# Layer 2's second modulation part: its eight pieces taken out of layer 1's merges and run between the two layers

## The chip, the cores and the metric

One Trainium2 chip, one core. The kernel is one program; the metric is its time on the device in microseconds, the median of several executions.

## What is computed

A diffusion backbone of two layers over 256 latent tokens and 256 context tokens, D = 1024. Each layer computes six modulation vectors, runs three token mixers behind one input projection, merges them by gates, and then a grouped mixture of 16 experts. Cut to what bears on this case:

```python
for l in range(DEPTH):
    ml = (silu(c) @ w_mod[l] + b_mod[l]).reshape(b, 1, N_MOD, d)          # w_mod[l]: 1024 x 6144
    mc = (silu(c_ctx) @ w_mod[l] + b_mod[l]).reshape(1, 1, N_MOD, d)
    hl = modulate(rms_norm(xl, norm1_g[l]), ml[:, :, 0], ml[:, :, 1])
    hc = modulate(rms_norm(xc, norm1_g[l]), mc[:, :, 0], mc[:, :, 1])
    out_l, out_c = token_mixers(hl, hc, w_in[l], ...)
    xl = xl + ml[:, :, 2] * out_l
    hl2 = modulate(rms_norm(xl, norm2_g[l]), ml[:, :, 3], ml[:, :, 4])
    ...
    f = grouped_moe(tokens, w_router, router_bias, w_gate_e[l], w_up_e[l], w_down_e[l])
    xl = xl + ml[:, :, 5] * f[:b * s].reshape(b, s, d)
    ...
```

The modulation depends on `c`, `c_ctx` and the weights alone, so layer 2's may be computed at any time before it is used.

## The kernel before

The layers are counted from 0 in the code: layer 1 of this text is `l == 0`, layer 2 is `l == 1`. Every engine has a program written out by hand (`block.sync` for SP, which issues the weight loads; `block.gpsimd`, `block.tensor`, `block.scalar`, `block.vector`), and they meet only in semaphores. Each engine does its list in order; a wait holds up all that stands behind it on that engine. SP loads weights chunk by chunk, 1 MB each, into a ring of three slots; the order of the chunks is a list (`order`), and `mod_behind` says behind which chunk a modulation piece is loaded.

**Modulation.** `w_mod` of a layer is 24 pieces of 128 x 2048 (1 MB), three parts (i = 0, 1, 2) of eight pieces (k = 0 to 7). Part 0 is shift and scale of the first norm, part 1 the gate of the mixers' output and the shift of the second norm, part 2 the scale of the second norm and the gate of the experts. A piece is `mod(l, i, k)` (L1032 to L1049): TensorE multiplies `csil` (silu of c and of c_ctx, 32 columns wide) with four blocks of 512 columns, into four row groups of one bank, and sums over k. Then ScalarE copies the bank (`mod_rows`), TensorE turns it by four transposes (`mod_columns`), VectorE adds the bias (`mod_take`). For layer 2 the pieces are loaded by `mod_piece` into places of their own (`mod_places`), mostly one buffer, `mod_next`, so that SP waits for `m_us` (pieces used) before it loads the next.

**Where layer 2's pieces run before.** In layer 1's merges. These are 3 branches (n) of 8 tiles (m). A tile is `gate` (8 steps over k, `mm3` = three products each, lines L1020 to L1022) and `branch` (4 steps), 36 products of 128x128 by 512 columns. `next_mod(1)` stands behind tiles 0, 3 and 7 of n = 0, behind all of n = 1 and behind the first five of n = 2: 16 pieces, part 0 and part 1. Part 2 follows behind the output projection and in the second norm.

**Experts and combine of layer 1.** After the last expert product, TensorE has work for layer 2's long filters: `filters`, `spectra_a`, `spectra_b` (products with `dft_f`, L1079 and L1097), and between them `keep_busy`, products of constants (`ones` by a constant table, L1011) whose results nobody reads. Meanwhile GpSimd gathers each token's first-choice rows (L908), stores the last expert's rows (L904), waits for all stores, signals `z_r`, and gathers the second-choice rows (L940): four gathers of 512 KB each, one for each 128 tokens. ScalarE scales the first choices, VectorE adds the second choices (L2909, `z_f`). TensorE then transposes the rows, column k into bank k (L1727); VectorE adds them to the stream `xT` (L2917, `z_x`), ScalarE squares, and TensorE sums the squares (L1004) for layer 2's first norm. Behind that stand `filters(l, 1)`, five more products of constants, and the first three tiles of layer 2's projection, run side by side (`in_bank`).

```python
                    spectra_b(l + 1, 0)
                    keep_busy(1, 5)
                    pe.wait_ge(f_a[l + 1], 6 * l + 10)
                pe.wait_ge(z_f[l], 4 * l + nt)
                pe.wait_ge(x_ya[l], 16 * l + NS)
                pe.wait_ge(x_yd[l], 16 * l + NS)
                for k in range(DK):
```

## Time and profile before

| | |
|---|---|
| median of 3 runs | 1567.48 us (1567.27 to 1571.9) |
| the profiled execution | 1569.26 us, its span 1567.6 us |
| TensorE busy | 1471.8 us, 94% of the span |
| VectorE, ScalarE, GpSimd | 877.5, 632.7, 406.1 us |
| DMA | 362.78 MB, mean 231 GB/s over the span |
| merges of layer 1 | about 362 to 510 us; out projection to 592 |
| last expert product of layer 1 | about 937 us |
| first projection product of layer 2 | 978.66 us |

How to read it: times are microseconds from the span's start. TensorE's products are pipelined, so their durations overlap and the distance from one start to the next is what a product costs. A row that starts with an engine's name and a line says what the engine did there, and behind it, in brackets, how long it had idled and whose work ended that. "PEclk" is the TensorE clock that was granted, as a share of 2.4 GHz. The DMA rows tell two queues apart: SP's (hardware) and GpSimd's (software); both use the same 16 DMA engines.

### The profile page before, as it was taken

The page shows a single profiled execution, that of the slowest core. Times are in us where ns is not written, and L with a number is a line of the kernel's source. Part 1 is how long each engine was busy: PE and PEld are TensorE (multiplying, and loading weights), DVE is VectorE, ACT ScalarE, POOL GpSimd, SP SyncE. Part 2 cuts the span into 40 slices and gives each one's busy share as a digit, 9 for nine tenths or more (in the row PEclk, how much of TensorE's full clock was granted, in tenths as well). Part 3 has the DMA queues.
Part 4 walks back from the last instruction along what each step waited for, and adds up shares of the span by engine and source line. Part 5 has one row for each costly group of instructions (what it writes and reads, how often), then busy time and mean ns, then how long its engine had stood idle before and what let it go on. Part 6 is the DMA issues. An engine that isn't in the chain of part 4 may idle for free.

```text
span 1567.6 us, 20695 instructions
## 1 busy us (share of the span) xinstructions
PE 1471.8 (94%) x8212; PEld 1086.9 (69%) x8212; DVE 877.5 (56%) x1266; ACT 632.7 (40%) x853; POOL 406.1 (26%) x367
## 2 busy tenths in 40 slices
PE   6999999899999997899999999999988997999997
PEld 2588788657777784678888874697868995445444
DVE  4725556774222347799999967664783566111112
ACT  2532222264222335477787755442264443010102
POOL 0446334201333440111101013473414661000000
PEclk9999999999999998899999999998999999999997
DMA  8423211376456573799999983252304766899993
GB/s 330 147 81 107 81 55 59 133 279 223 160 191 205 190 277 126 267 370 403 406 409 405 397 314 122 65 185 81 102 22 152 259 233 276 329 420 420 422 421 133
DMA packets 116898, 362.78 MB, mean 231 GB/s; under 512 B 7774, under 2 KB 73632, under 8 KB 85952
## 3 DMA queue, kind: packets, MB, share of 16 engines
q1 hardware_dynamic: 109296, 334.62, 56.5%
q0 software_dynamic: 7504, 26.81, 4.6%
q8 instruction: 67, 1.10, 0.3%
q14 instruction: 31, 0.25, 0.0%
HBM read 349.86 MB, written 11.53 MB: 231 GB/s over the span
## 4 chain that ended last, share of the span: by engine, by line
PE 49%; DVE 10%; issue 2%; ACT 1%; DMA 0%; POOL 0%; DVEq 0%; PEldq 0%; ACTq 0%
PE bank L1020 9%; PE bank L1021 9%; PE bank L1022 9%; PE bank L1540 7%; PE bank L1579 4%; PE bank L1493 2%; PE bank L1479 1%; PE bank L1549 1%; PE bank L1504 1%; PE bank L1097 1%; PE bank L1231 1%; PE bank L1606 1%; PE bank L1011 1%; PE bank L1607 1%; DVE mix L2403 0%
## 5 line engine op out<-in xcount | busy, mean ns | idle before, releaser
L833 POOL TENSOR_TENSOR w_lo<-ring,w_hi 128x256 fp32r<-128x256 f32 (+1 forms) x300 | 347.8, 1188 | 515.0 <-ACT w_hi L1864 515.0
L1020 PE MATMUL bank<-h_hi,w_hi 128*128 128x512 f32 (+1 forms) x768 | 272.1, 354 | 8.8 <-POOL w_lo L833 3.4
L1021 PE MATMUL bank<-h_hi,w_lo 128*128 128x512 f32 (+1 forms) x768 | 263.1, 343 | 0.0
L1022 PE MATMUL bank<-h_lo,w_hi 128*128 128x512 f32 (+1 forms) x768 | 263.0, 342 | 0.0
L1020 PEld LDWEIGHTS bank<-h_hi,w_hi 128*128 128x128 f32 x768 | 146.5, 191 | 41.1 <-issue 16.5
L1021 PEld LDWEIGHTS bank<-h_hi,w_lo 128*128 128x128 f32 x768 | 146.6, 191 | 16.8 <-issue 1.4
L1022 PEld LDWEIGHTS bank<-h_lo,w_hi 128*128 128x128 f32 x768 | 146.5, 191 | 16.8
L1020 PE MATMUL bank<-w_hi,h_hi 128*128 128x512 f32 (+1 forms) x384 | 141.8, 369 | 6.7 <-DVE h_lo L2785 3.1
L1864 ACT ACTIVATE w_hi<-ring 128x1024 fp32r<-128x1024 f32 x120 | 125.4, 1052 | 40.5 <-PE bank L1020 31.4
L1021 PE MATMUL bank<-w_hi,h_lo 128*128 128x512 f32 (+1 forms) x384 | 138.1, 360 | 0.0
L1022 PE MATMUL bank<-w_lo,h_hi 128*128 128x512 f32 (+1 forms) x384 | 137.7, 359 | 0.0
L2561 DVE SCALAR_TENSOR_TENSOR mix<-mix,bank 128x512 f32<-128x512 f32 (+1 forms) x48 | 26.5, 553 | 168.5 <-PE bank L1022 116.7
L1020 PEld LDWEIGHTS bank<-w_hi,h_hi 128*128 128x128 f32 x384 | 74.1, 193 | 17.7 <-issue 3.7
L2043 ACT ACTIVATE mix<-bank 128x256 f32<-128x256 f32 (+1 forms) x39 | 18.8, 481 | 165.9 <-PE bank L1022 164.2
L2617 DVE TENSOR_TENSOR w_lo<-ring,w_hi 128x2048 fp32r<-128x2048 f32 x32 | 73.3, 2292 | 17.4 <-ACT w_hi L2073 17.4
L1022 PEld LDWEIGHTS bank<-w_lo,h_hi 128*128 128x128 f32 x384 | 74.0, 193 | 10.8
L1021 PEld LDWEIGHTS bank<-w_hi,h_lo 128*128 128x128 f32 x384 | 74.1, 193 | 10.4 <-issue 0.5
L2617 DVE TENSOR_TENSOR w_lo<-mix,w_hi 128x2048 fp32r<-128x2048 f32 x32 | 73.1, 2284 | 2.3 <-ACT w_hi L2073 2.3
L2073 ACT ACTIVATE w_hi<-mix 128x2048 fp32r<-128x2048 f32 x32 | 61.4, 1918 | 22.1 <-PE bank L1022 22.1
L994 POOL TENSOR_SCALAR mix<-xT,fin_g 128x256 f32<-128x256 f32 x4 | 3.6, 919 | 253.8 <-DVE xT L2917 253.8
L2073 ACT ACTIVATE w_hi<-ring 128x2048 fp32r<-128x2048 f32 x32 | 61.2, 1915 | 19.3 <-PE bank L1022 19.3
L1540 PE MATMUL bank<-operands_plain,mix 128*64 128x512 f32 x248 | 63.9, 594 | 0.0
(367 smaller groups left out, 2865.6 us busy)
## 6 DMA issues: line engine op xcount, KB each, us to landing
ring<-in_w_in SPq DMA_DIRECT2D x52, 1024.0 KB, 5.0
mix<-in_w_gate_e SPq DMA_DIRECT2D x40, 1024.0 KB, 7.8
ring<-in_w_up_e SPq DMA_DIRECT2D x38, 1024.0 KB, 8.1
mix<-in_w_down_e SPq DMA_DIRECT2D x25, 1024.0 KB, 8.3
ring<-in_w_mod SPq DMA_DIRECT2D x24, 1024.0 KB, 6.0
ring<-in_w_down_e SPq DMA_DIRECT2D x23, 1024.0 KB, 7.5
mix<-in_w_mod SPq DMA_DIRECT2D x19, 1024.0 KB, 4.9
operands_plain<-in_w_up_e SPq DMA_DIRECT2D x16, 1024.0 KB, 12.3
```

The source lines that it names most:

```text
L833: last = pool.tensor_tensor(w_lo[:, slot, k:k + n], rview(raw, 8)[:, k:k + n, x * P:(x + 1) * P], w_hi[:, slot, k:k + n].bitcast(F32), ALU ...
L1020: first = mm(dst, stat[0], mov[0], start=start, stop=False)
L1021: mm(dst, stat[1], mov[0], start=False, stop=False)
L1022: return first, mm(dst, stat[0], mov[1], start=False, stop=stop)
L1493: last = mm(bank[i][:, k * P:(k + 1) * P], htok[:, j, (4 * i + k) * P:(4 * i + k + 1) * P], hot_rows[l][e % 2][:, j, :], start=j == 0, sto ...
L1540: last = mm(dst[x * M:(x + 1) * M, :], heT[:, 0, 4 * h + k, x * M:(x + 1) * M], raw(l, c)[:, k * FF:(k + 1) * FF], start=h + k == 0, stop= ...
L1579: last = mm(y_bank[o][x * M:(x + 1) * M, :], hidT[:, 0, 2 * h + k, x * M:(x + 1) * M], raw(l, c)[:, k * D + o * 512:k * D + (o + 1) * 512] ...
L1864: A(w_hi[:, slot], rview(raw, 8)[:, :, x * P:(x + 1) * P], ACT.Copy).then_inc(w_h, 1)
L2043: A(gate_t[:, m % 2, 0:T], gate_v, ACT.Tanh, scale=0.5).then_inc(g_t[l], 1)
L2073: A(xhi[c % XH], raw(0, c), ACT.Copy).then_inc(x_wh, 1)
L2561: last = V.scalar_tensor_tensor(gated, gate_t[:, m % 2, 0:T], 1.0, bank[2 + m % 2][:, 0:T], ALU.add, ALU.mult)
L2617: V.tensor_tensor(xlo[c % XH], raw(0, c), xhi[c % XH].bitcast(F32), ALU.subtract).then_inc(x_wd, 1)
```

## The change

Part 1 of layer 2 no longer runs in layer 1's merges. The order of the parts becomes 0, 2, 1 (`nth`). In the merges, n = 1 keeps pieces behind its first five tiles, n = 2 has none. Six pieces of part 1 take the place of the five products of constants before the row transposes; two more stand behind `filters(l, 1)`, where five products of constants become three. The part's eight loads (`late_piece`, nine DMAs) stand in SP's list behind layer 2's first three ring chunks: the first four wait for the last expert product of layer 1 (`x_u`), the fifth for `z_r`, the seventh for the sixth to be used. They land in `plain` (the area of the operands), `mix` and `mod_next`. Since the part now holds bank 6 until layer 2's first tiles are done, the third tile goes to bank 7, the sizes of the second filter to bank 5, and row column 6 to bank 1, behind a wait for VectorE. ScalarE's copy stands behind layer 2's first norm, the four transposes behind the third tile, VectorE's add behind the taps.

```diff
@@ -302,7 +302,9 @@
         ropes = [v.rearrange("p (i t) -> p i t", i=2) for v in rope_at]
         tidx = sb("tidx", [P, 64], U32)
 
-        mod_places = ([mod_next] * (2 * DK) + [ahead[:, 0:2048], mod_next] + [plain[:, 2048 * i:2048 * (i + 1)] for i in range(4)]
+        late_places = [[plain[:, 2048 * i:2048 * (i + 1)]] for i in (1, 3, 0, 2)]
+        late_places += [[area(0, 2048)], [mod_next], [mod_next], [plain[:, o + 3072:o + 4096] for o in (8192, 12288)]]
+        mod_places = ([mod_next] * DK + late_places + [ahead[:, 0:2048], mod_next] + [plain[:, 2048 * i:2048 * (i + 1)] for i in range(4)]
                       + [area(o, 2048) for o in (4096, 8192)])
         didx = sb("didx", [P, 2, 4], U32)
         counts = sb("counts", [P, 8], U32)
@@ -487,12 +489,23 @@
             return mods[:, i:i + n, s] if l == 0 else mods_next[:, MOD_T * s + i:MOD_T * s + i + n]
 
         def transforms_to(l):
-            return 16 * (4 + l * (2 + MOD_C))
+            return 16 * (4 + l * (2 + 2 * DK))
 
         def acc(k):
 
             return bank[4 + k // 2][:, k % 2 * SEQ:(k % 2 + 1) * SEQ]
 
+        def nth(l, i):
+
+            return 3 * l + (0, 2, 1)[i] if l else i
+
+        def late_sem(j):
+
+            return j % len(x_full)
+
+        def late_to(j):
+            return 16 * (EXP_C // len(x_full) + j // len(x_full) + 1)
+
         def mbank(l, i):
 
             return bank[7 if l == 0 and i else 5 + i % 2]
@@ -505,9 +518,17 @@
 
             return 6 + v % 2 * l
 
-        def in_bank(g):
-
-            return bank[6 if g == 2 else g % 2]
+        def in_bank(l, g):
+
+            return bank[6 + l if g == 2 else g % 2]
+
+        def size_bank(l, o):
+
+            return bank[5 if l and o else 7]
+
+        def row_bank(k):
+
+            return bank[1 if k == 6 else k]
 
         fbank = [[bank[i] for i in (2, 3, 4, x)] for x in (0, 5)]
 
...
@@ -730,7 +752,7 @@
             def mod_piece(p):
 
                 if p:
-                    sp.wait_ge(m_us, min(p, 2 * DK))
+                    sp.wait_ge(m_us, min(p, DK))
                 else:
                     sp.wait_ge(a_o[0], len(units_of[0]))
                 if p == 3 * DK - 1:
@@ -739,10 +761,22 @@
                 sp.dma_start(mod_places[p], a["w_mod"][1, k * P:(k + 1) * P, i * RW:(i + 1) * RW]).then_inc(s_lds, 16)
 
 
+            def late_piece(j):
+
+                if j == 0:
+                    sp.wait_ge(x_u, EXP_C)
+                elif j == 4:
+                    sp.wait_ge(z_r, 1)
+                elif j == 6:
+                    sp.wait_ge(m_us, 2 * DK + j)
+                n = RW // len(late_places[j])
+                for i, place in enumerate(late_places[j]):
+                    sp.dma_start(place, a["w_mod"][1, j * P:(j + 1) * P, RW + i * n:RW + (i + 1) * n]
+                                 ).then_inc(x_full[late_sem(j + i)], 16)
+
             base = at_of[("out", 0, 0)] - MERGE_C
             mod_behind = {base + 4: [0, 1], base + 6: [2], base + 8: [3], base + 9: [4, 5, 6],
-                          base + 11: [7], base + 12: [8, 9, 10], base + 14: [11], base + 15: [12, 13, 14],
-                          base + 17: [15], base + 18: [16, 17], base + 21: [18, 19, 20, 21, 22, 23]}
+                          base + 11: [7], base + 18: [16, 17], base + 21: [18, 19, 20, 21, 22, 23]}
 
 
             once_behind = (6, 9, 12)
@@ -783,6 +817,9 @@
                         filter_tables(l + 1)
                     for p in mod_behind.get(at, []):
                         mod_piece(p)
+                    if l and at == lo + RS - 1:
+                        for j in range(DK):
+                            late_piece(j)
                     if l and kind == "merge" and i in once_behind:
                         expert_load(l, once_behind.index(i))
                 for c in range(len(once) if l else 0, EXP_C):
...
@@ -1037,14 +1074,20 @@
 
                     pe.wait_ge(j_a[l], TAKEN)
                 if l:
-                    pe.wait_ge(s_lds, transforms_to(0) + 16 * (DK * i + (DK if i == 2 else k + 1)))
+                    if i == 1:
+                        for j in range(k, k + len(late_places[k])):
+                            pe.wait_ge(x_full[late_sem(j)], late_to(j))
+                    else:
+                        pe.wait_ge(s_lds, transforms_to(0) + 16 * (2 * DK if i else k + 1))
                     w = mod_places[DK * i + k]
+                    w = w if isinstance(w, list) else [w]
                 else:
                     at = at_of[("mod", l, DK * i + k)]
                     pe.wait_ge(ring_full[at % RS], full_at(at))
-                    w = ring[:, at % RS]
+                    w = [ring[:, at % RS]]
+                n = 4 // len(w)
                 for c in range(4):
-                    last = mm(mbank(l, i)[32 * c:32 * c + 32, :], csil[:, k, :], w[:, c * 512:(c + 1) * 512],
+                    last = mm(mbank(l, i)[32 * c:32 * c + 32, :], csil[:, k, :], w[c // n][:, c % n * 512:(c % n + 1) * 512],
                               start=k == 0, stop=k == DK - 1)
                 last.then_inc(m_us if l else ring_used, 1)
 
...
@@ -1137,13 +1180,15 @@
                         norm_sum(2 * l, NT, k)
                     pe.wait_ge(z_x[l - 1], 16 * l)
                     filters(l, 1)
-                    keep_busy(6, 5)
+                    keep_busy(1, 3)
+                    for k in range(DK - 2, DK):
+                        mod(l, 1, k)
 
                 def proj_steps(g):
 
                     cols = NT if 20 <= g < 24 else T
                     q = g if g < 24 else g - 4
-                    b = in_bank(g) if g < 12 else bank[g % 4 if g < 16 else 6 + g % 2]
+                    b = in_bank(l, g) if g < 12 else bank[g % 4 if g < 16 else 6 + g % 2]
                     abreast = g < ABREAST[l]
 
                     pe.wait_ge(w_l, q0 + q + 1)
@@ -1202,6 +1247,8 @@
                     if g >= ABREAST[l]:
                         proj_tile(g)
                     if g == 2:
+                        if l:
+                            mod_columns(l, 1)
                         spectra_a(l, 1)
                     if g == 3 - l:
                         spectra_b(l, 1)
@@ -1353,12 +1400,11 @@
                             first.then_inc(carry, 1)
                     last.then_inc(g_pe[l], done)
 
-                pieces = [0]
+                pieces = iter([(i, k) for i in (0, 2, 1) for k in range(DK)])
 
                 def next_mod(n):
-                    for p in range(pieces[0], pieces[0] + n):
-                        mod(1, p // DK, p % DK)
-                    pieces[0] += n
+                    for _ in range(n):
+                        mod(1, *next(pieces))
 
                 pe.wait_ge(a_o[l], U)
                 for n in range(3):
@@ -1382,10 +1428,10 @@
                         else:
                             branch(n, m, 1)
                             gate(n, m, g_pe[l], ring_used)
-                        if l == 0 and (n == 1 or m % 4 == 3 and n == 0 or n == 2 and m < 5):
+                        if l == 0 and (n == 1 and m < 5 or n == 0 and m % 4 == 3):
                             next_mod(1)
-                        if l == 0 and n and m == 6:
-                            mod_columns(1, n - 1)
+                        if l == 0 and n == 1 and m == 6:
+                            mod_columns(1, 0)
                     if n == 0 and l == 0:
                         pe.wait_ge(j_pe[l], 32 + DK)
                     else:
@@ -1712,7 +1758,8 @@
                     keep_busy(1, 4)
                     spectra_a(l + 1, 0)
                     spectra_b(l + 1, 0)
-                    keep_busy(1, 5)
+                    for k in range(DK - 2):
+                        mod(l + 1, 1, k)
                     pe.wait_ge(f_a[l + 1], 6 * l + 10)
 
                 if l:
@@ -1721,10 +1768,12 @@
                 pe.wait_ge(x_ya[l], 16 * l + NS)
                 pe.wait_ge(x_yd[l], 16 * l + NS)
                 for k in range(DK):
+                    if k == 6:
+                        pe.wait_ge(z_x[l], 16 * l + 4)
                     if k == DK - 1 and l + 1 < DEPTH:
                         pe.wait_ge(f_d[l + 1], 10 * l + 16)
                     for j in range(nt):
-                        last = tp(bank[k][:, j * P:(j + 1) * P], fa[j][:, k * P:(k + 1) * P], ident)
+                        last = tp(row_bank(k)[:, j * P:(j + 1) * P], fa[j][:, k * P:(k + 1) * P], ident)
                     last.then_inc(z_t[l], 1)
 
             rows_bank = [bank[2:4], bank[4:6]]
...
@@ -1877,6 +1926,8 @@
                     spectrum_b(l, 0)
                 act.wait_ge(m_d[l], 2 * l + 1)
                 norm_act_scale(2 * l, NT, 2)
+                if l:
+                    mod_rows(1, 1)
 
                 for g in range(12):
                     if g + AHEAD >= ABREAST[l]:
...
@@ -2357,12 +2408,14 @@
                 if l == 0:
                     gate_scales(0, 0)
                 taps(l, 1)
+                if l:
+                    mod_take(1, 1)
 
                 for g in range(12):
                     dve.wait_ge(j_c[l], 12 * l + g + 1)
                     dst = hv[:, g, 0:T] if g < 4 else hx[:, (g - 4) // 4, g % 4, 0:T]
                     dst = dst.rearrange("p (s t) -> p s t", t=SEQ)
-                    src = in_bank(g)[:, 0:T].rearrange("p (s t) -> p s t", t=SEQ)
+                    src = in_bank(l, g)[:, 0:T].rearrange("p (s t) -> p s t", t=SEQ)
                     link(V.scalar_tensor_tensor(dst[:, :, 1:SEQ], src[:, :, 0:SEQ - 1], pc[:, C_TAP + g:C_TAP + g + 1],
                                                 dst[:, :, 1:SEQ], ALU.mult, ALU.add))
                     V.scalar_tensor_tensor(dst[:, :, 0:SEQ - 1], src[:, :, 1:SEQ],
...
```

TensorE, from layer 2's first spectra to the first row transpose, before (L1011 are the products of constants, L1727 the transposes):

```order
L1092 MATMUL bank<-square,mix 128x1 x7
L1097 MATMUL bank<-mix,dft_f 128x512 [waits filter_act]
L1097 MATMUL bank<-mix,dft_f 128x512 x3
L1011 MATMUL bank<-square 128x512 x5
L1727 MATMUL bank<-square,gates_ahead 128x128 [waits expert_out_first,expert_out_second,combined,filter_act]
```

and with the change (L1090 is a piece, L1776 the transposes; `mix` and `operands_plain` are places of pieces):

```order
L1135 MATMUL bank<-square,mix 128x1 x7
L1140 MATMUL bank<-mix,dft_f 128x512 [waits filter_act]
L1140 MATMUL bank<-mix,dft_f 128x512 x3
L1090 MATMUL bank<-operands_plain,csil 32x512 [waits expert_weights_loaded0]
L1090 MATMUL bank<-operands_plain,csil 32x512 x3
...
L1090 MATMUL bank<-mix,csil 32x512 [waits expert_weights_loaded4]
L1090 MATMUL bank<-mix,csil 32x512 x3
L1090 MATMUL bank<-mix,csil 32x512 [waits expert_weights_loaded5]
L1090 MATMUL bank<-mix,csil 32x512 x3
L1776 MATMUL bank<-square,gates_ahead 128x128 [waits expert_out_first,expert_out_second,combined,filter_act]
```

Five products that wait for nothing have become six pieces, each of which waits for its load.

SP, at the start of its part for layer 2, before:

```order
L715 DMA mix<-in_hy_w 128x1024
L716 DMA mix<-in_decay 128x1024
L779 DMA ring<-in_w_in 128x8x256 [waits expert_weights_split]
L728 DMA poolw<-in_pool_w 128x4x128
L779 DMA ring<-in_w_in 128x8x256 [waits expert_weights_split] x2
L779 DMA ring<-in_w_in 128x8x256 [waits weight_half_split] x13
```

and with the change:

```order
L813 DMA ring<-in_w_in 128x8x256 [waits expert_weights_split] x2
L774 DMA operands_plain<-in_w_mod 128x2048 [waits expert_weights_used]
L774 DMA operands_plain<-in_w_mod 128x2048 x3
L774 DMA mix<-in_w_mod 128x2048 [waits expert_rows_all_stored]
L774 DMA mix<-in_w_mod 128x2048
L774 DMA mix<-in_w_mod 128x2048 [waits mod_piece_used]
L774 DMA operands_plain<-in_w_mod 128x1024 x2
L813 DMA ring<-in_w_in 128x8x256 [waits weight_half_split] x13
```

The nine loads stand between the third ring chunk and the fourth.

## Rows read from the trace of the kernel before

**Rows 1.** The page: TensorE's busy time, share of the span, instructions.

```profile
PE 1471.8 (94%) x8212; PEld 1086.9 (69%) x8212; DVE 877.5 (56%) x1266; ACT 632.7 (40%) x853; POOL 406.1 (26%) x367
```

**Rows 2.** Windows, merges of layer 1: length; PE, PEld, DVE, ACT, POOL; clock, DMA.

```profile
430.00:512.00 82.00, 82.00 (x389) 59.61 (x388) 19.97 (x25) 19.01 (x26) 26.62 (x32) 1.00 0.61 206
```

**Rows 3.** Timeline of PE, merges: start, duration, engine, line; L1047 pieces, L1029 transposes.

```profile
425.91 1.07 PE L1047 MATMUL bank<-mix,csil 128*32 128x512 f32 x8
...
435.30 1.07 PE L1047 MATMUL bank<-mix,csil 128*32 128x512 f32 x8
...
463.46 1.07 PE L1047 MATMUL bank<-mix,csil 128*32 128x512 f32 x8
464.45 0.66 PE L1029 MATMUL bank<-square,mix 128*128 128x128 f32 x4
...
473.24 1.07 PE L1047 MATMUL bank<-mix,csil 128*32 128x512 f32 x8
```

**Rows 4.** Timeline of PE, last expert product to layer 2's projection.

```profile
938.01 1.99 PE L1070 MATMUL bank<-mix 64*128 64x512 f32 x8 [0.75 <-PE bank L1022]
...
955.24 4.46 PE L1011 MATMUL bank<-square 128*128 128x512 f32 x10
959.53 0.49 PE L1727 MATMUL bank<-square,gates_ahead 128*128 128x128 f32 x3
...
963.06 7.70 PE L1004 MATMUL bank<-mix,square 128*128 128x512 f32 x16
...
972.61 4.56 PE L1011 MATMUL bank<-square 128*128 128x512 f32 x10
978.66 0.36 PE L1020 MATMUL bank<-h_hi,w_hi 128*128 128x256 f32 x1 [1.49 <-DVE h_lo L2254]
```

**Rows 5.** Timeline of POOL and DVE in the combine.

```profile
939.88 0.59 POOL L904 DMA_DIRECT2D y_rows<-mix  x1
947.32 1.60 POOL L940 DMA_INDIRECT mix<-y_rows,didx  x1 [6.84 <-DMA y_rows<-mix]
...
957.81 1.28 DVE L2909 SCALAR_TENSOR_TENSOR mix<-mix,wsel 128x1024 f32<-128x1024 f32 x1
...
961.46 6.36 DVE L2917 SCALAR_TENSOR_TENSOR xT<-bank,mods,xT 128x256 f32<-128x256 f32 x16
```

**Rows 6.** DMA queues (records, MB, engine share): 937-939.4, 939.4-957.5, 949.5-957.5, 874-876 us.

```profile
q0 software_dynamic: 180, 0.67, 94.4%
q0 software_dynamic: 1110, 4.02, 66.1%
q0 software_dynamic: 576, 2.10, 80.2%
q0 software_dynamic: 110, 0.42, 58.1%
q1 hardware_dynamic: 59, 0.37, 45.7%
```

**Rows 7.** Windows, SP's queue alone (last: GB/s); DMA issues, median us to landing.

```profile
554.00:558.00 4.00, 4.00 (x19) 3.06 (x18) 0.05 (x1) 1.66 (x2) 4.00 (x7) 1.00 1.03 427
...
mix<-in_w_mod SPq DMA_DIRECT2D x19, 1024.0 KB, 4.9
...
operands_plain<-in_w_mod SPq DMA_DIRECT2D x4, 1024.0 KB, 12.2
...
mix<-y_rows,didx POOLq DMA_INDIRECT x4, 5.8
```

**Rows 8.** Windows at the low clock (third number from the end), and spectra at either.

```profile
930.00:933.50 3.50, 3.50 (x9) 2.78 (x10) 0.00 (x0) 0.00 (x0) 0.00 (x0) 0.53 0.65 242
...
991.00:995.00 4.00, 3.90 (x5) 1.65 (x6) 3.97 (x3) 0.93 (x2) 4.00 (x2) 0.57 0.14 29
...
944.48 3.70 PE L1079 MATMUL bank<-mix,dft_f 128*128 128x512 f32 x8 [0.85 <-DVE mix L2316]
...
991.10 5.40 PE L1079 MATMUL bank<-mix,dft_f 128*128 128x512 f32 x8 [1.85 <-DVE mix L2316]
```

29 lines of the change are left out of this document (15 added, 14 removed).

## Prediction

> **What bounds the kernel now.** I read the page first, then the merges of layer 1 engine by engine, then the stretch between layer 1's last expert and layer 2's first projection, and last the DMA queues there, since the change takes work out of the first place and puts it into the second.
>
> TensorE is busy 94% of the span [rows 1]. In the merges, where the eight pieces of the second part run today, it is busy 82.00 of 82.00 us, while VectorE, ScalarE and GpSimd have 20, 19 and 27 us [rows 2]. So what is taken out there is gained in full. The reader should see in the timeline that one merge tile with a piece behind it takes 9.39 us (425.91 to 435.30), and that the tile which also has the four transposes behind it takes 9.78 (463.46 to 473.24) [rows 3].
>
> In the combine there are two chains. TensorE's own: last expert product before 938.0, the spectra, five products of constants (955.24, 4.46 us), then the row transposes at 959.53 and the sums of squares at 963.06 [rows 4]. Beside it the rows' chain: GpSimd stores the last expert rows (939.88), may gather the second choices only when all is stored (947.32), VectorE adds the last of them from 957.81 to 959.09, and the transposes wait for that [rows 5]. So TensorE's filling and the gathered rows end within half a microsecond of each other: either is the bound as soon as it grows. The DMA engines carry 0.67 MB of GpSimd's queue from 937 to 939.4 and 4.02 MB from 939.4 to 957.5, and nothing of note from SP's queue [rows 6]. That is the empty place that the change wants to fill.
>
> **Taken out of layer 1's merges.** A merge tile is 36 products, at the spacing of 0.227 us that the tile of 9.39 us leaves when a piece is set at 1.22: 36 x 0.227 = 8.17, and 9.39 - 8.17 = 1.22 us [rows 3]. Eight pieces are 9.76 us, and the four transposes 9.78 - 9.39 = 0.39 more: **-10.15 us**. I count it whole, since no other engine has even a third of the time there [rows 2]. ScalarE's copy, VectorE's add, and eight loads of 1 MB leave the stage too; nothing waited for them, so they give nothing. SP's ring loads are no longer queued behind the waits for these pieces, which gives nothing either where TensorE never idles.
>
> **Put into the combine: TensorE.** Six pieces in place of five products of constants. A piece is four narrow products side by side, 1.07 us from first to last [rows 3], 0.9 when they follow each other; a product of constants is 4.46 / 5 = 0.89 [rows 4]. That is 0.9 to 2 us more. It costs nothing of its own if the rows' chain has grown by more than that, which the next paragraph says. The last two pieces stand where two of the five products before the first projection stood (972.61, 4.56 us), and TensorE is 1.49 us early there [rows 4], so they are free as long as they have landed. They are issued once the sixth is used, and the sums of squares (7.7 us) and more lie in between, against 4.9 us to land [rows 4, 7].
>
> **Put into the combine: DMA.** This is the term that decides. SP may start the first four pieces when the last expert product is done, 937.3; with 4.9 us to land, of which 1.05 / 0.427 = 2.5 are transfer, their bytes begin at 939.7 [rows 4, 7]; the rows are split at 939.4, and I count from there. The fifth and the sixth go out with the signal that all rows are stored, which is also the gathers' start. All six, 6 x 1.05 = 6.29 MB, must have landed before the row transposes, because TensorE takes its work in order; the gathers must too. The order in which the two queues are served hardly matters, then: the later of them ends when 4.02 + 6.29 = 10.31 MB are through the same sixteen engines. What rate? GpSimd's queue alone keeps the engines over 90% busy at 0.28 MB/us (0.67 MB in 2.4 us) [rows 6]; SP's queue alone reaches 0.427 [rows 7]; where both run, as from 874 to 876, 0.42 and 0.37 MB pass in 2 us, 0.395 MB/us, with each queue holding about half of the time [rows 6]. This last row is the nearest, and I take it: 10.31 / 0.395 = 26.1 us, to 965.5. The bounds are 10.31 / 0.427 = 24.1 us (963.5) and 4.02 / 0.28 + 6.29 / 0.427 = 29.1 us (968.5). The last rows landed, 0.3 us for the signal, 1.28 for VectorE's add and 0.44 to the first transpose, as today [rows 4, 5], put the transposes at 967.5 instead of 959.53: **+8.0 us**, bounds 6.0 and 11.0.
>
> **The bank moved.** Row column 6 now goes into bank 1, which VectorE must have emptied. It starts its sixteen adds 1.93 us after the first transpose and takes 0.4 us for each [rows 4, 5], so four are done at +3.5; the two last columns (3.53 / 8 = 0.44 us each) follow, and the sums of squares start at +4.5 instead of +3.53: **+1.0 us**. Were the pieces last to land, not the rows, VectorE would be ahead and this would be 0.
>
> **The clock.** TensorE will wait for rows and for the sixth piece. Rows of both levels exist here: from 930 to 933.5 and from 991 to 995, the latter after TensorE had idled 1.85 us, the granted clock was 0.53 and 0.57, that is 1.2 GHz nearly all the time; the same eight products took 5.40 us at 991 in place of 3.70 at 944 [rows 8]. A second cause of idling: ScalarE scales the first-choice rows before it copies the spectra out, and TensorE's second spectra wait for that copy; first choices that land late will hold them up. At the transposes part of such a loss falls on time in which they wait for VectorE anyway. I take **+1.0 us**, between 0 and 4 (the sums of squares, 7.7 us at full clock, half of them at the low one).
>
> **Edits priced at nothing.** ScalarE's copy of the part stands after the norm, where it has nothing to do until the first tiles are done; the four transposes after the third tile stand in the 1.85 us in which TensorE waits for VectorE at 991.10 [rows 8]; VectorE's add of 16 numbers a partition stands before its first convolution, while TensorE runs the second spectra. SP's next ring chunk goes out behind the pieces, and its slot comes free only when GpSimd has split two halves, about when the sixth piece is used. Were these covers gone, the transposes would cost 0.39 us as in the merges, the copy and the add less than 1 us together.
>
> **Sum.** -10.15 + 8.0 + 1.0 + 1.0 = -0.15 us. The profiled execution took 1569.26 us, 1.8 more than the median of 1567.48; the difference is applied to the median: 1567.3, which I give as 1567.4. A measurement of this kernel can tell 0.3%, 4.7 us, from no change; so the forecast is **no change**.
>
> **The rule on the queues.** The rows show each queue with about half of the engines' time: 58% and 46% from 874 to 876, and GpSimd's 110 records of 3.8 KB against SP's 59 of 6.3 [rows 6]. The Trainium skill, DMA: Bandwidth & Descriptors, section "Queues, rings and completion order", says that an engine goes round the queues packet by packet, a packet being a group of descriptors. By that rule the share would go by the packets' sizes and not be a half; the row bears it out only in so far as neither queue is starved. It is rival B below.
>
> **Rivals.** A, faster: the DMA engines are not as full as they look, and the two queues together reach SP's 0.427 MB/us. Then the pieces end last, at 963.5 (bound above), the transposes start at 965.0 (+5.5), the bank wait and the clock cost nothing, and if the four transposes keep the clock at the spectra at 991, 1.7 us come back: -10.15 + 5.5 - 1.7 = -6.3 us, 1561. For it: the share column counts time in which a packet is under way, not bytes. Against it: wherever both queues run, the rows give 0.395. A weaker kind, in which the gathers are not touched at all and only TensorE's extra microsecond counts, would give -8.
>
> B, slower: the gathers are starved. If GpSimd's queue gets a third of the bytes while SP's has work, its first 4.02 - 2.10 = 1.92 MB [rows 6] take until 954, the gathers start at 958 instead of 950 with the engines empty for about 2 us in between, and they end at 969, transposes at 971: +11.5. TensorE has then used five pieces and idles for several microseconds, so the transposes and half of the sums of squares run at 1.2 GHz, +3.5, and the bank adds 1.0: -10.15 + 16.0 = +5.9 us, 1573.3. It decides from a share of about 0.4 downward, with the clock low; with a full clock it stays within the bound. For it: loads that are queued several deep take 12.2 us to land, not 4.9, and gathers land in 5.8 today with nobody beside them [rows 7]. Against it: the halves in the row.
>
> C: the change does not do what it says, because something else takes the merges' time. Rows 2 leave no engine for that; 0.02.
>
> **Chances.** Forecast (a sum within 4.7 us of zero) 0.66; A 0.14, of which 0.12 beyond the bound; B 0.18; C 0.02, which would cost the sum without its saving and so be slower. Where the sum's bounds are taken at their ends, -10.15 + 6.0 + 0 = -4.2 and -10.15 + 11.0 + 1.0 + 4.0 = +5.9. So the range is 1562.5 to 1573.5; it reaches into A and B and leaves about 2 in 10 out. Faster 0.12, same 0.66 + 0.02 = 0.68, slower 0.18 + 0.02 = 0.20.
>
> **What would show it.** Merge tiles of 8.17 us and the last merge product about 10 us earlier; SP's queue with some 6 MB between the last expert product and the transposes; second-choice gathers taking over 8 us to land instead of 5.8; the transposes some 30 us after the last expert product, not the 22 us of today; sums of squares 4.5 us after the first transpose; an idle TensorE before the sixth piece. The prediction is wrong if the second choices land within 3 us of today's distance (then it is faster), or if the granted clock from the transposes to the first projection is mostly 0.5 (then it is slower).

## The result, and the profile after

The change made the kernel slower: 1578.43 us in the median of five runs (1575.42 to 1584.45) against 1567.51 for the kernel before on the same chip, a ratio of 1.0066 (95% interval 1.0049 to 1.0083). Run again later beside other kernels it took 1574.88 us in the median of ten runs, against 1568.47: 1.0043 (1.0025 to 1.0061). So the loss is some 6 to 11 us, where the forecast was none, and both results lie outside the range of 1562.5 to 1573.5.

All numbers below that come from "the profile after" are of one execution of 1578.43 us with a span of 1576.8. The merges gave what they should. In the windows of layer 1's merges TensorE is still busy nearly all the time (81.69 of 82.00 us), as in [rows 2], now without the part's pieces:

```profile
430.00:512.00 82.00, 81.69 (x368) 65.43 (x367) 23.88 (x29) 24.06 (x31) 29.23 (x37) 1.00 0.44 148
```

The sum of norm 2 behind the merges starts at 584.6 us, at 594.6 before: 10.0 us earlier. The combine lost it again. TensorE's timeline there, which answers to [rows 4] (L1113 are the filters' first products, L1140 the second spectra, L1090 the pieces, L1776 the row transposes, L1041 the sums of squares):

```profile
925.55 1.99 PE L1113 MATMUL bank<-mix 64*128 64x512 f32 x8 [0.77 <-PE bank L1059]
...
944.46 5.54 PE L1140 MATMUL bank<-mix,dft_f 128*128 128x512 f32 x8 [5.05 <-ACT mix L1879]
949.93 3.64 PE L1090 MATMUL bank<-operands_plain,csil 128*32 128x512 f32 x32
953.38 1.90 PE L1090 MATMUL bank<-mix,csil 128*32 128x512 f32 x16
963.65 0.87 PE L1776 MATMUL bank<-square,gates_ahead 128*128 128x128 f32 x3 [8.37 <-issue]
...
969.62 7.60 PE L1041 MATMUL bank<-mix,square 128*128 128x512 f32 x16
```

The reader should see two idle stretches that were not there: 5.05 us before the second spectra, and 8.37 us between the sixth piece and the first transpose. The first is the second cause of idling that the prediction named: the first-choice rows reach ScalarE late, at 939.18, and the copy of the spectra stands behind them. It does not set the transposes, since TensorE has done its six pieces 8.37 us before them. The transposes start 38.1 us after the first filter product, 21.5 before [rows 4]. "issue" names no one for the 8.37 us, since TensorE waits for several signals there; the timelines of POOL, DVE and SP's queue tell who it was, and answer to [rows 5]:

```profile
926.65 0.59 POOL L941 DMA_DIRECT2D y_rows<-mix  x1
944.44 0.97 POOL L977 DMA_INDIRECT mix<-y_rows,didx  x1 [17.20 <-DMA y_rows<-mix]
...
952.66 9.80 POOL L870 TENSOR_TENSOR w_lo<-ring,w_hi 128x1024 fp32r<-128x1024 f32 x3 [3.54 <-ACT w_hi L1913]
...
952.39 7.88 DVE L2962 SCALAR_TENSOR_TENSOR gates_ahead<-mix,wsel,gates_ahead 128x1024 f32<-128x1024 f32 x3 [16.61 <-DMA mix<-y_rows,didx]
960.19 3.35 DVE L2962 SCALAR_TENSOR_TENSOR mix<-mix,wsel 128x1024 f32<-128x1024 f32 x1
...
924.82 2.01 SPq L774 DMA_DIRECT2D operands_plain<-in_w_mod  x4
943.69 11.98 SPq L774 DMA_DIRECT2D mix<-in_w_mod  x3
```

The store of the last expert rows was issued at 926.65 and was there 17 us later (6.84 before), so the gathers of the second choices start 18.9 us after the first filter product instead of 9.3. And VectorE's adds take 2.6 us each, the last one 3.35, where one took 1.28; they lie beside GpSimd's splits of layer 2's first weights. The DMA queues, which answer to [rows 6], from 928 to 940 us (both at work), from 942 to 946, and from 946 to 955.6 us (after the queue's name: records, MB, share of the engines):

```profile
q1 hardware_dynamic: 427, 3.13, 66.4%
q0 software_dynamic: 419, 1.53, 33.6%
...
q1 hardware_dynamic: 63, 0.41, 37.7%
q0 software_dynamic: 6, 0.01, 0.8%
...
q0 software_dynamic: 576, 2.10, 53.6%
q1 hardware_dynamic: 252, 1.80, 44.7%
```

In the first stretch each queue passes as many records as the other, 427 and 419; SP's are 7.3 KB in the mean, GpSimd's 3.7, so that GpSimd gets a third of the bytes. In the second, SP's four loads are through, nobody may start the next transfers before the store's signal, and 0.42 MB pass in 4 us. In the third, the sums hide a sequence: SP's queue is alone from 946 to 948 (0.84 MB), GpSimd's from 952 to 954 (0.84 MB), so these counts say nothing of how the two share.

**Where the time went**, by distances between the same products in the two profiles: merges -10.0; from norm 2's sum to the first filter product -2.4 (340.9 us against 343.4; the other profiles of kernels with the change have 341.0 to 344.2, so this is scatter); first filter product to the end of the norm's sums 51.1 against 32.2, +18.9; from there to the last product with the pooling weights 89.6 against 87.9, +1.7; the rest +1.1. The sum is +9.3, and the last transpose starts at 1571.2 instead of 1561.9.

### The profile page after: what moved, and what is told of

The parts are those of the page before. It is cut to its first block and busy times, and to the rows that moved or that the text cites. A ratio compares the mean times of both kernels' runs of the same rounds, so it can differ in the third digit from the quotient of the medians.

```text
span 1576.8 us, 20669 instructions
## 1 busy us (share of the span) xinstructions
PE 1466.6 (93%) x8198; PEld 1088.0 (69%) x8198; DVE 878.3 (56%) x1266; ACT 632.8 (40%) x853; POOL 406.6 (26%) x367
## 5 line engine op out<-in xcount | busy, mean ns | idle before, releaser
L1057 PEld LDWEIGHTS bank<-h_hi,w_hi 128*128 128x128 f32 x768 | 146.6, 191 | 37.7 <-issue 12.2
L1913 ACT ACTIVATE w_hi<-ring 128x1024 fp32r<-128x1024 f32 x120 | 125.4, 1053 | 45.9 <-PE bank L1057 31.4
```

What stands on the lines that cost most here:

```text
L1057: first = mm(dst, stat[0], mov[0], start=start, stop=False)
L1913: A(w_hi[:, slot], rview(raw, 8)[:, :, x * P:(x + 1) * P], ACT.Copy).then_inc(w_h, 1)
```

## The experiments

All times of a run are compared with the kernel before on the same chip. Since medians of one kernel differ by a few us between chips, the distance in the profile from the first filter product to the first row transpose (before 21.5, changed 38.1) and to the end of the norm's sums (before 32.2, changed 51.1) tells more; both are given for each. "Norm's end" is the start of the last product of these sums.

### The yardstick: the changed kernel once more

> The changed kernel itself once more, on the chip of the two runs beside it, so that all experiments have a yardstick: 1577 to 1579, norm's end 50 to 52 us after the first filter product, adds of the second choices at 2 to 3.4 us, the store landing after 17 us. If it is at 1573 or less here, the gains of single edits are the chip's and not theirs.

1574.88 us (1569.75 to 1580.81) against 1568.47. Transposes at 37.7, norm's end at 51.2, adds of 1.96 (5.89 for three) and 3.35 us, the store waited for 18.3 us. Both distances repeat within 0.4 us, but not what they are made of: the DMA engines fell idle at 955.7, 31.4 us after the first filter product (29.9 in the profile after), and the transposes started 6.3 us behind that instead of 8.2. The median is 3.5 us lower than in the first measurement. It is above 1573, but below the 1577 that I expected, so single gains of 2 us can't be read from medians here.

### Next to no bytes, and half of them

The first leaves all waits, all pieces and all transposes in place and takes the bytes away.

```
-                    sp.dma_start(place, ...RW + i * n:RW + (i + 1) * n])
+                    sp.dma_start(place[:, 0:16], ...RW + i * n:RW + i * n + 16])
...
+                    w = [dft_f[:, 0, :]] * 4 if i == 1 else w
```

> The changed kernel, but each late load fetches 16 columns of its piece instead of 2048 (the products of this part take a constant in place of the weights, so layer 2's second modulation part is left out). All else stands: waits, pieces, transposes, the splits beside the adds. Theory 1 (the combine lost by the loads' bytes and by what they make late): the store lands after 7 us again, the transposes start 22 to 24 us after the first filter product (21.5 before the change, 38.1 with it), and the whole is 8 to 10 us below the kernel before, 1558 to 1560: the merges' 10.15 less about one. Theory 2 (a part of the loss is TensorE's longer work or the moved bank, whatever is loaded): the norm's end stays 4 us or more behind 32.2, the whole at 1564 or more. If the adds stay beside the splits and take 2.6 us or more even without the loads, they were slow by their place and not by the bytes; I expect 1.28, since the splits begin only after them.

```profile
936.43 1.57 POOL L977 DMA_INDIRECT mix<-y_rows,didx  x1 [7.16 <-DMA y_rows<-mix]
...
947.01 1.28 DVE L2963 SCALAR_TENSOR_TENSOR mix<-mix,wsel 128x1024 f32<-128x1024 f32 x1
...
947.17 8.02 POOL L870 TENSOR_TENSOR w_lo<-ring,w_hi 128x1024 fp32r<-128x1024 f32 x3 [5.43 <-ACT w_hi L1914]
```

Transposes at 22.6, norm's end at 33.2: 1.0 us more than before, for six pieces in place of five products of constants, the bank and all waits. The adds are at 1.28 us, and the last begins just ahead of the splits. So 17.9 of the 18.9 us hang on the loads' bytes, directly or by what they delay. The whole took 4199.79 us, which I had not expected: with another gate, layer 2 seems to send its tokens to its experts in another way (the trace has 144 loads of expert weights of 2 MB that the kernel before has not), and everything behind its router tells nothing. My 1558 to 1560 can't be read from it; the norm's end at 960.3 us, 9.9 before that of the kernel before, is the nearest that there is.

> The changed kernel, but each late load fetches the first half of its columns, 4 KB a record (the products of this part take a constant, so layer 2's second modulation part is left out; layer 2 then routes its tokens in another way, and only the stretch up to its projections can be compared). The transposes came 22.6 us after the first filter product with next to no bytes and 38.1 us with 6.29 MB. Theory 1 (what counts is the bytes beside GpSimd's queue, each megabyte 2.5 us of the engines' time): 3.15 MB cost half, transposes at 29 to 31 us. Theory 2 (the first loads hide in gaps, and the loss begins only with the last ones): at 26 us or less. The adds are at 1.28 us if they end before the splits begin, above 2 if they fall beside them.

Transposes at 29.6, norm's end at 40.2, the adds at 1.26 in the mean of the first three and 1.29 for the last. Half of the bytes cost 7.0 us, about 2.2 us a megabyte, near the 2.5 of theory 1, though these loads also differ from the change's by their records of 4 KB. The second half costs 8.5, in part because with it the adds fall beside the splits: where the splits are moved away (the next run), it costs 4.6. Both queues passed 473 records from 929 to 939 us, 1.71 and 1.72 MB.

### The adds and the splits

```
+                if l:
+                    pool.wait_ge(z_f[0], 4)
                 for q in range(early):
                     trail_ahead(q)
```

> The changed kernel, with one wait more: GpSimd begins to split layer 2's projection weights only when all four tiles of rows are combined, not beside VectorE's last adds. Theory 1 (the adds of the second-choice rows, 2.6 to 3.35 us each instead of 1.28, are slowed by GpSimd's splits of 9.8 us beside them): each add is back at 1.3 to 1.5 us, the row transposes start some 5 us earlier, 33 to 34 us after the last expert product instead of 38.9, and the whole takes about 1573, provided that the splits, now later, do not hold up the first projections (three splits of 8 us each against some 20 us from the transposes to the first projection: a close thing). Theory 2 (the adds wait for their rows, whose landing is late; their length is only the wait seen from inside): the adds stay at 2.6 or more, the transposes stay at 38 to 39 us, the whole at 1578.

```profile
944.23 0.96 POOL L979 DMA_INDIRECT mix<-y_rows,didx  x1 [18.52 <-DMA y_rows<-mix]
...
952.19 3.84 DVE L2964 SCALAR_TENSOR_TENSOR gates_ahead<-mix,wsel,gates_ahead 128x1024 f32<-128x1024 f32 x3 [18.73 <-DMA mix<-y_rows,didx]
955.99 1.28 DVE L2964 SCALAR_TENSOR_TENSOR mix<-mix,wsel 128x1024 f32<-128x1024 f32 x1
...
957.37 7.01 POOL L870 TENSOR_TENSOR w_lo<-ring,w_hi 128x1024 fp32r<-128x1024 f32 x3 [8.45 <-DVE mix L2964]
```

1572.25 us (1.0018, 1.0001 to 1.0035); transposes at 34.2, norm's end at 46.3. The adds are back at 1.28 us with the same waits for the same rows: theory 1. The DMA engines are at work beside them until 955.1, so it was not the transfers that slowed the adds. In the profile after, the DMA engines fell idle at 955.4 and the transposes started 8.2 us behind that, here 2.3 us (955.1 and 957.4). The store was even later here (18.5 us), so the gain is 3.9 us at the transposes instead of 6; at the norm's end it is 4.8.

### When the first four loads go out

```
                 if j == 0:
                     sp.wait_ge(x_u, EXP_C)
-                elif j == 4:
                     sp.wait_ge(z_r, 1)
```

> The changed kernel, but the first four of the late loads also wait until the last expert rows are stored, as the fifth and sixth do. Theory 1 (what counts is the sum of 10.31 MB through one set of engines, with a gap of about 2 us while nobody had work; the order hardly matters): the store lands after 7 us again instead of 17, the second-choice gathers are issued at 18 us after the last expert product less 8, but then share the engines with six loads from start to end, so that all is landed 28 to 30 us after the last expert product instead of 30.8, the transposes at 36 to 38 instead of 38.9, and the whole gains 1 to 3 us, 1576 to 1577. Theory 2 (the harm was done by the third of the bytes that the store and the first choices get): the gathers of the second choices get their third now instead, 2.10 MB at 0.14 MB/us are 15 us, so that the rows land last, and nothing is gained: 1578 to 1580.

1572.59 us (1.0022, 1.0010 to 1.0034); the store is there after 7.25 us, the first add starts 19.7 us after the first filter product instead of 26.8; transposes at 34.6, norm's end at 45.9. The gain was 5.2 us where theory 1 had 1 to 3 and theory 2 none, and neither has its source. The empty stretch of the DMA engines did not shrink: it stands between the store and the gathers here too, only earlier (0.43 MB from 935.6 to 939.6). Nor are the bytes through sooner: all but 14 records have passed at 959.1, 30.8 us after the first filter product, against 29.9 in the change. And the gathers do get a third, as theory 2 said. From 944 to 958 us:

```profile
q1 hardware_dynamic: 549, 3.97, 67.7%
q0 software_dynamic: 536, 1.94, 34.2%
```

What is gained lies behind the bytes. The rows come one by one, and VectorE is not behind when the last ones come: its adds still take 3.12 and 2.67 us where they fall beside the splits, but each has 3.7 us until the next rows. The transposes start 3.8 us after 959.1, not 8.2, which is 3.5 us earlier by the first filter product; the other 1.7 us are gained between the first transpose and the norm's end. TensorE now waits for the pieces (1.80 to 2.68 us before three of them), and the sixth ends as the transposes start.

### SP's records halved

Each late load was made two of 1024 columns.

> The changed kernel, with each late load of 2048 columns made two of 1024, so that SP's records are 4 KB like those of GpSimd's queue. Theory 1 (the engines take a record of each queue in turn, whatever its size, so 8 KB against 4 KB left the gathers a third of the bytes): from 928 to 940 GpSimd's queue gets 0.19 to 0.21 MB/us instead of 0.13 to 0.15, the store lands some 3 to 4 us earlier than 17 us after its issue, the engines' empty stretch after it shrinks or goes, and the transposes come 1 to 3 us earlier. If smaller records also lower the engines' rate (0.395 to 0.36 MB/us), half of that is lost. Theory 2 (the share is not by records; SP's queue, being ahead by four whole loads, takes what it takes): the shares stay a third and two thirds, and the distances stay the same.

The DMA queues of this run, from 927 to 937 us, and from 929 to 935 us, where both had work all the time:

```profile
q1 hardware_dynamic: 551, 2.02, 54.6%
q0 software_dynamic: 457, 1.68, 45.3%
...
q1 hardware_dynamic: 312, 1.14, 50.3%
q0 software_dynamic: 303, 1.12, 50.2%
```

In the longer window GpSimd's queue got 0.168 MB/us instead of 0.128 (1.53 in 12 us), and the store was there after 12.8 us instead of 17.2. In the inner six microseconds the records are equal and GpSimd's queue gets 0.187 MB/us; the 551 to 457 come from the ends of the longer window (107 records to 51 from 927 to 929, 132 to 103 from 935 to 937). So the size of SP's records sets the share: theory 1. The empty stretch is gone too, since SP's loads now last beyond the store: its queue alone fills 99.4% of the engines from 937 to 942. But the two queues together fell from 0.39 to 0.37 MB/us. Transposes at 33.8, norm's end at 47.1, 4.0 us better than the change; but the median is 1577.05 us (1.0055, 1.0036 to 1.0075), and the 4 us do not show in it. Its four runs cannot tell it from the changed kernel.

### TensorE kept busy before the transposes

Eight products of constants behind the sixth piece.

> The changed kernel, with eight products of constants between the sixth late piece and the row transposes, where TensorE idled 8.37 us. Theory 1 (that idling cost the clock: first transposes 0.85 us a column against 0.49, sums of squares 5.97 us after the first transpose instead of 3.53): the eight products (7.1 us at full clock) lie within the idle time, the transposes start where they did and take 0.49 us again, and the norm's end comes about 2.4 us earlier, 1576. Theory 2 (the transposes are slow because each waits for VectorE's adds or for the bank): their spacing stays at 0.7 or more with the granted clock at 1, and nothing is gained: 1578.

```profile
956.65 7.13 PE L1048 MATMUL bank<-square 128*128 128x512 f32 x16
963.62 0.49 PE L1777 MATMUL bank<-square,gates_ahead 128*128 128x128 f32 x3
...
967.12 7.60 PE L1041 MATMUL bank<-mix,square 128*128 128x512 f32 x16
```

The transposes take 0.49 us again, and the sums of squares start 3.50 us after the first of them instead of 5.97. The norm's end comes 10.5 us after the first transpose instead of 13.0: 2.5 us of the loss were the clock (the granted clock of the changed kernel from 963.4 to 969.6 was 0.57). It also shows that the wait for bank 1 costs nothing here, since 3.5 us is what the kernel before had. Transposes at 38.8, norm's end at 49.3. In the whole, 1576.94 us (1.0063, 1.0038 to 1.0088), nothing can be seen of 2 us.

### Three edits, and two

> The changed kernel with three edits tried singly before: the first four loads wait for the stored rows, GpSimd's splits wait for the combined rows, and eight products of constants stand before the row transposes. Singly they brought the norm's end, counted from the first filter product after the last expert, from 51.1 us to 45.9, 46.3 and 49.3 (32.2 before the change). Theory 1 (the bytes, 10.31 MB at 0.395 MB/us, are now the floor): the rows are still all landed only some 31 us after the last expert product, so the two first gains do not add; transposes 33 to 34 us after the first filter product, norm's end at 43.5 to 45, the whole 1570 to 1572. Theory 2 (the losses are separate and add): 51.1 - 5.2 - 4.8 - 1.8 = 39.3 us, the whole about 1566.

1578.40 us (1.0060, 1.0040 to 1.0080): both theories missed. The norm's end was at 53.0 us, later than without any edit.

```profile
961.84 1.94 PE L1091 MATMUL bank<-mix,csil 128*32 128x512 f32 x8 [0.82 <-DMA mix<-in_w_mod]
963.70 7.97 PE L1049 MATMUL bank<-square 128*128 128x512 f32 x16
```

With the loads sent out later, the sixth piece is used just before the rows are ready, and the eight products of constants stand behind it: they no longer fill a wait, they are one. The rows were combined at 961.3 and the transposes started at 971.5. That was my mistake in composing the kernel: the filling had been measured where TensorE idled.

> The changed kernel with two edits together: the first four loads wait for the stored rows, and GpSimd's splits wait for the combined rows. Without the eight products of constants, which in the kernel with three edits stood behind the sixth piece and delayed the transposes by their own 8 us. Theory 1 (with the loads sent at the stored rows, the sixth piece's landing and not the adds sets the transposes): nothing is gained over the loads' edit alone, transposes 34 to 35 us after the first filter product, the whole about 1572. Theory 2 (the adds set them): 2 to 4 us earlier, about 1569.

1570.53 us (1.0018, 1.0003 to 1.0032), measured beside the 1574.88 of the changed kernel; transposes at 34.1, norm's end at 45.8, 0.1 us better than with the loads' edit alone. Adds of 1.28 us, 2.5 us idle before each: the rows arrive every 3.75 us, and the sixth piece, used from 958.56, takes 1.94 us and the first transpose follows at 960.4. Theory 1: here the bytes themselves are the bound, and the part in the combine stays above the kernel before.

### The pieces elsewhere, the loads as in the change

> The kernel with the pieces behind the norm's sums, but with the loads sent out as in the change (four at the last expert product, two at the stored rows). It tells what the loads alone do to the combine, since TensorE has no piece there. Theory 1 (the bytes and the third left to GpSimd's queue make the loss, not TensorE's waiting in order): the store lands after 17 us, the second choices land as late as in the change, transposes 36 to 38 us after the first filter product, adds at 2.6 to 3.4 us beside the splits; the whole 1575 or more. Theory 2 (TensorE's order, with the sixth piece ahead of the transposes, made the loss): the transposes come 5 us or more earlier than in the change, 33 us or less, and the whole stays under 1571.

1578.26 us (1.0074, 1.0052 to 1.0096); transposes at 36.7, norm's end at 48.7, the store after 17.0, adds of 1.95 and 3.35 us. With no piece in TensorE's way the combine is nearly as slow as in the change. Theory 1: the loads did it, not the order of TensorE's work.

### The pieces elsewhere, and the loads behind the gathers

The combine is as before, with its five products of constants and row column 6 in its own bank; six pieces follow the sums of squares, where five products of constants stood; two more follow projection tile 3, and ScalarE's copy and the four transposes go behind them. The main lines of the edit:

```
+                    for k in range(DK - 2):
+                        mod(l, 1, k)
                     filters(l, 1)
-                    keep_busy(1, 3)
-                    for k in range(DK - 2, DK):
-                        mod(l, 1, k)
...
                 if j == 0:
                     sp.wait_ge(x_u, EXP_C)
-                elif j == 4:
                     sp.wait_ge(z_r, 1)
+                    for t in range(NT // P):
+                        sp.wait_ge(z_g[t], 16)
```

> Another place for the part: the combine is as before the change (five products of constants, no extra load beside the gathers, no bank wait); the first six pieces stand behind the sums of squares of layer 2's norm, where five products of constants and an idle stretch of 1.49 us were, the seventh and eighth before the second filter's spectra after the third projection tile, where TensorE idled 1.85 us; their loads go out only when the second choices have landed. Theory 1 (TensorE has 4.56 us of products of constants and some idle time there, the DMA engines are empty from the transposes on, and nothing else waits): the merges' 10 us stay won; six pieces take 5.5 to 6 us in place of 6.05 (products of constants and idling), the last two about 2 us in place of 1.85: -10.15 + 0.5 + 0.4 = -9.2, so about 1559 to 1560 where before takes 1569. Theory 2 (loads issued at the last gather's landing are not there 10.7 us later, and the first projection waits for them: 6.3 MB at 0.427 MB/us are 14.7 us): TensorE waits 3 to 4 us for the fifth and sixth piece, 1562 to 1564.

```profile
945.32 4.46 PE L1051 MATMUL bank<-square 128*128 128x512 f32 x10
...
953.11 7.60 PE L1044 MATMUL bank<-mix,square 128*128 128x512 f32 x16
960.63 3.64 PE L1093 MATMUL bank<-operands_plain,csil 128*32 128x512 f32 x32
964.09 1.90 PE L1093 MATMUL bank<-mix,csil 128*32 128x512 f32 x16
```

and its window from 948 to 962 us, with 420 GB/s of loads beside a TensorE that never idles:

```profile
948.00:962.00 14.00, 14.00 (x69) 6.93 (x71) 7.08 (x18) 8.74 (x13) 7.02 (x3) 1.00 1.00 420
```

**1557.26 us (1554.96 to 1560.2) against 1566.88: a ratio of 0.9929 (0.9913 to 0.9944), 9.6 us faster than the kernel before**, where theory 1 had 9.2. Transposes at 21.5, norm's end at 32.0, and 87.9 us from there to the last product with the pooling weights, as before the change. Between this and the run ahead of it stands nothing but the moment at which the loads go out: the first four 18.1 us after the first filter product instead of 0.7 before it, the next two 1.4 us later than there. The six pieces wait for nothing: the loads start at 946.2, 6.29 MB at 0.42 MB/us are 15.0 us, and the fifth piece begins at 964.1. Theory 1.

## Why the prediction was wrong

**The merges** (-10.15): right. -10.0 in the profile.

**Pieces in place of constants, the last two free, the copy, add and transposes covered**: right; with next to no bytes the whole of this costs 1.0 us at the norm's end.

**"The order in which the two queues are served hardly matters"**: this step failed first. The amount (10.31 MB) and the rate while both run (0.39 MB/us, 4.66 MB in 12 us) were right. But the step supposed that there would always be something to move. Between the store's last bytes and the gathers' first ones GpSimd's queue is empty, before the change as well (two records, under 0.01 MB, from 946.1 to 949.6 us). The four loads were to fill that stretch; but while SP's queue is full GpSimd's gets a third of the bytes, so the store took 17 us in place of 7, SP's four loads ended before it, and for 4 us 0.42 MB moved, which is worth 2.9 us (4 less 0.42 / 0.395). The DMA engines fell idle 29.9 us after the first filter product, where the forecast had 27.5: +2.4 (+3.9 in the repeat). For the end of the bytes alone the order mattered little, since the run with the loads at the stored rows has 30.8; what the order sets is when each row comes. I had this as rival B, at 0.18, and spoke against it with the halves of [rows 6]. Those were halves of time in one stretch of 2 us with 110 records against 59, where GpSimd's queue was not held back; why not, no row tells. The record counts of the profile after, 419 to 427, are the better reading. The Trainium skill, DMA: Bandwidth & Descriptors, section "Queues, rings and completion order", has each engine go round the queues packet by packet, a packet being several descriptors. The equal counts agree with it if a record of the profile is one packet, which no run here shows. With SP's records halved the store came 4.4 us earlier.

**"The last rows landed, 0.3 us for the signal, 1.28 for VectorE's add and 0.44 to the first transpose, as today"**: this failed too, and in the profile after it failed most. 8.2 us in place of 2.0: **+6.2 us** (6.3, or +4.3, in the repeat, where the two failures are of one size). The adds of the kernel before were short because all of them had begun before GpSimd's first split; the last is at 957.81 [rows 5], and the splits of that profile begin at 958.07. The splits do not wait for the second-choice rows. Counted from the first filter product the splits came 7.0 us later with the change (27.1 us instead of 20.1), the first add 12.5 us later (26.8 instead of 14.3), and so the adds fell beside them. I asked what hides TensorE's work and never what VectorE would find beside it. It is shown by the run in which the splits wait for the rows (2.3 us). The Trainium skill, SBUF — State Buffer, section "SBUF: two separate sides", says that a GpSimd operation that reads SBUF and a VectorE operation with two inputs in SBUF take turns for a pair of ports, each for a whole instruction. The trace agrees roughly: four adds of 1.28 and three splits of 2.34 (7.02 in the last experiment, where no such add is near) are 12.1 us in turns, and the stretch took 11.15 (952.39 to 963.54), where side by side they could be done in 7.0 to 7.9.

**The moved bank** (+1.0): did not exist. The sums start 3.50 us after the first transpose when the clock is full. The forecast let VectorE's adds to `xT` begin 1.93 us after the first transpose, as before. But what held them up there was one small operation beside the first split:

```profile
959.41 1.94 DVE L2330 TENSOR_TENSOR par<-par,small 128x16 f32<-128x16 f32 x1
```

With the change the same operation takes 0.18 us, the splits being over, and the adds begin 1.19 us after the first transpose; in the run with TensorE kept busy it is done before the transposes, and they begin 0.71 us after.

**The clock** (+1.0): 2.5 at the norm. Together with the bank the sum had 2.0, and 2.3 was measured, so this part of the sum came out right by two errors.

**Behind the norm** (0): +1.7 us that the sum did not have. TensorE has its full clock at the first spectra (3.70 us), as hoped, but waits 2.33 us before the sizes and does these and the second spectra slowly:

```profile
1005.40 2.86 PE L1135 MATMUL bank<-square,mix 128*128 128x1 f32 x16 [2.33 <-DVE mix L2372]
```

The four transposes before the first spectra lengthen nothing (the idle time is 1.42 in place of 1.85), and the time won in the spectra is spent at the next wait. In the run with the splits moved the wait is the same 2.33 us, the sizes take 1.95 and nothing is lost (87.9 us to the last pooling product, as in the kernel before and all other runs but two; the changed kernel's repeat and the run with halved records have 89.6). The granted clock in this stretch is 0.85 in the change, in its repeat and with halved records, and 0.92 with the splits moved, so the loss goes with the clock; why it fell in some and not in the others stays open.

In sum: the transposes came 8.6 us later than forecast (2.4 + 6.2), and the rest by 0.3 at the norm and 1.7 behind it. With -2.4 (scatter) and +1.1 elsewhere, -0.15 becomes +9.3. Rival B had the sign and the queues' part of the mechanism, and with 1573.3 us missed VectorE's part. The losses don't add when they are repaired: the splits' edit gave 4.8 us, the loads' edit 5.2, both 5.3, since behind either stand the bytes.

## What to carry to other kernels

An empty DMA stretch beside small, serial transfers (a store, its signal, then gathers) is not free space: what a bulk load costs there is set by who needs its bytes first, and large records on one queue push the small ones of another to a fraction. Send the bulk when the last of the dependent transfers has landed, and look for a place for its use that much later; here this turned 6 to 11 us lost into 9.6 won.

When a step is made later, ask for every engine on its way what it will then run beside; a duration read from a trace holds only for the company it had. And work that fills an idle stretch must stand where the idle stretch is in that very kernel.

## What the runs showed of the hardware

Two queues passed nearly equal numbers of records while both had several transfers waiting, whatever their sizes: 427 and 419 in the profile after, 549 and 536 with the loads at the stored rows, 312 and 303 with halved records, 473 and 473 with half loads. The bytes then go by the records' sizes: 67% to 33% with 7.3 KB against 3.7. The 2 us before the change with 59 and 110 [rows 6] do not fit, and stay unexplained.

A VectorE add of 128 x 1024 with its inputs in SBUF takes 1.28 us alone and up to 3.37 beside a GpSimd operation of two inputs, and a small operation of 128 x 16, of 0.18 us, takes 1.94 beside the splits; the smaller adds from a bank into `xT` keep 0.4 us each [rows 5], though the splits of that profile last until 966.0.

Idle time of 8.37 us left TensorE at a granted clock of 0.57 for the next 6.2 us; with products of constants up to the transposes it was 1.00.
